# Two layers of a hybrid attention and mixture-of-experts trunk: when VectorE takes up layer 0's conditioning vectors, and in which PSUM bank they wait

## The reference, cut to what matters

```
m = silu(cvec) @ w_ada[li] + b_ada[li]          # split into 6 vectors of 1024
h = rmsnorm(y, g_pre_mix[li]) * (1 + m[1]) + m[0]
u = h @ w_in[li]                                # 1024 x 2560: q, k, v of both attentions, pool
y = y + m[2] * rmsnorm(attention_and_pool(u) @ w_out[li], g_post_mix[li])
h = rmsnorm(y, g_pre_ffn[li]) * (1 + m[4]) + m[3]
y = y + m[5] * rmsnorm(moe(h), g_post_ffn[li])  # 64 routed experts, top 8, and a shared one
```

## Time and profile before

| | |
|---|---|
| median of 3 runs | 1432.21 us (1431.74 to 1433.58) |
| profiled execution | 1431.63 us, of which its span 1429.8 us |
| TensorE busy | 1344.9 us, 94% of the span |
| VectorE busy | 466.5 us, 33% |
| ScalarE busy | 334.3 us, 23% |
| mean DMA rate | 348 GB/s |
| granted TensorE clock, mean | 0.972 of full |

### The profile page before, as it was taken

The page is one execution under the profiler, slowest core; times in us unless marked ns, Lnnn a source line. Parts: engine busy times, 40 slices in busy tenths (PEclk is TensorE's granted clock), DMA queues, the critical chain, the costliest instruction groups (busy, mean ns, idle before and its releaser), DMA issues.

```text
span 1429.8 us, 30290 instructions
## 1 busy us (share of the span) xinstructions
PE 1344.9 (94%) x12298; PEld 734.1 (51%) x12298; DVE 466.5 (33%) x1110; ACT 334.3 (23%) x594; POOL 64.7 (5%) x89
## 2 busy tenths in 40 slices
PE   3859989999999999999989998999999999999996
PEld 2646755445444544544547875544454454454453
DVE  0514754222222222222237375422222222222223
ACT  1413551111111111111134365111111111111111
POOL 0210020000000000000013102000000000000000
PEclk9889989999999999999999998999999999999999
DMA  9878465999999999999966846599999999999990
GB/s 368 330 297 334 174 251 200 396 404 412 398 406 412 393 418 401 404 401 405 409 235 222 323 175 260 195 385 416 410 394 417 408 401 400 412 408 403 398 410 31
DMA packets 86294, 497.42 MB, mean 348 GB/s; under 512 B 7728, under 2 KB 7728, under 8 KB 36336
## 3 DMA queue, kind: packets, MB, share of 16 engines
q1 hardware_dynamic: 84416, 491.58, 85.8%
q0 software_dynamic: 1840, 5.31, 1.0%
HBM read 494.24 MB, written 2.62 MB: 347 GB/s over the span
## 4 chain that ended last, share of the span: by engine, by line
PE 88%; DMA 3%; DVE 3%; ACT 2%; issue 1%; SPq 1%; POOL 1%; ACTq 0%; POOLq 0%
PE PS L877 31%; PE PS L908 16%; PE PS L852 12%; PE PS L680 9%; PE PS L869 9%; DMA weights<-in_w_in 3%; PE PS L701 2%; PE PS L820 2%; PE PS L896 1%; PE PS L841 1%; ACT weights_split L983 1%; PE PS L772 1%; SPq L388 1%; DVE h L1213 1%; PE PS L859 1%
## 5 line engine op out<-in xcount | busy, mean ns | idle before, releaser
L877 PE MATMUL PS<-weights,gathered 128*32 128x512 f32 (+1 forms) x3968 | 451.3, 592 | 0.0
L877 PEld LDWEIGHTS PS<-weights,gathered 128*32 128x32 f32 (+1 forms) x3968 | 133.6, 111 | 306.3 <-issue 306.3
L908 PE MATMUL PS<-weights,hiddenT 128*32 128x512 f32 (+1 forms) x1984 | 233.0, 595 | 0.0
L852 PEld LDWEIGHTS PS<-pick,x_parts 128*128 128x128 bf16 x3168 | 177.2, 98 | 54.7 <-issue 54.7
L852 PE MATMUL PS<-pick,x_parts 128*128 128x128 bf16 x3168 | 188.3, 219 | 0.0
L1538 DVE SCALAR_TENSOR_TENSOR hidden<-PS,slot_gate,silu 128x256 f32<-128x256 f32 x64 | 30.9, 484 | 397.8 <-ACT silu L1103 397.8
L1110 ACT ACTIVATE y_hi<-PS 128x512 fp32r<-128x512 f32 x128 | 76.5, 598 | 295.8 <-PE PS L908 295.8
L1548 DVE TENSOR_TENSOR y_lo<-PS,y_hi 128x512 fp32r<-128x512 f32 x128 | 88.5, 692 | 140.2 <-ACT y_hi L1110 140.2
L1103 ACT ACTIVATE silu<-PS 128x256 f32<-128x256 f32 x64 | 24.6, 384 | 417.5 <-PE PS L877 417.5
L908 PEld LDWEIGHTS PS<-weights,hiddenT 128*32 128x32 f32 (+1 forms) x1984 | 60.5, 110 | 116.0 <-issue 114.6
L680 PE MATMUL PS<-weights_split,hT_high 128*128 128x512 f32 x448 | 111.5, 403 | 7.7 <-ACT hT_high L964 6.1
(11 more groups left out here) (268 smaller groups left out, 952.8 us busy)
## 6 DMA issues: line engine op xcount, KB each, us to landing
weights<-in_w_gate SPq DMA_DIRECT2D x128, 1024.0 KB, 7.7
weights<-in_w_up SPq DMA_DIRECT2D x128, 1024.0 KB, 11.6
weights<-in_w_down SPq DMA_DIRECT2D x128, 1024.0 KB, 9.2
weights<-in_w_ada SPq DMA_DIRECT2D x24, 2048.0 KB, 13.8
weights<-in_w_in SPq DMA_DIRECT2D x9, 2048.0 KB, 11.2
weights<-in_w_out SPq DMA_DIRECT2D x4, 2048.0 KB, 10.3
weights<-in_w_in SPq DMA_DIRECT2D x2, 1024.0 KB, 24.2
weights<-in_ws_gate SPq DMA_DIRECT2D x2, 1024.0 KB, 5.5
```

What stands on the lines that cost most here:

```text
L852: last = mm(PS[:, 5 + half, j * P:(j + 1) * P], x3[:, g, part, jj, :], pick[:, u % 2, g, 0:P], start=(g, part) == (0, 0), stop=(g, part) = ...
L877: last = mm(PS[a:z, 4, :].rearrange("p (a n) -> p a n", a=2), xgT[:, b, j, a:z], w[:, e, :, j, :], start=j == 0, stop=j == KT - 1, tile_po ...
L908: last = mm(PS[a:z, bank, :], hidT[:, j, a:z], w[:, e, j, n * HALF:(n + 1) * HALF], start=j == 0, stop=j == FT - 1, tile_position=(0, a), ...
```

## The change

Three edits. In the in-projection loop the vector after block n goes to bank n % 2 and not to bank 0: (0,2) to bank 1, (0,3) to bank 0, (0,4) to bank 1. VectorE's `finish_vector` stands ahead of the low part of block n + 1 and reads the matching bank. The head transposes at the start of attention, which write banks 0 and 1, wait for the latest vector begun, not for the latest in bank 0; for layer 0 both are the fifth.

```diff
@@ attention(l), TensorE
-                if 0 in last_in:
-                    pe.wait_ge(mod_ready, last_in[0])
+                if AFTER_BLOCK[l]:
+                    pe.wait_ge(mod_ready, started[0])
                 heads_out(0, range(8), 0, 0)
@@ in-projection loop, TensorE
                     if n in AFTER_BLOCK[l]:
-                        modulate(AFTER_BLOCK[l][n], 0)
+                        modulate(AFTER_BLOCK[l][n], n % 2)
@@ in-projection loop, VectorE
                 for n in range(5):
+                    if n - 1 in AFTER_BLOCK[l]:
+                        finish_vector((n - 1) % 2)
                     if n < 4:
                         low_weights(l, "in", n + 1)
                     if l == 0 and n == 2:
                         lambda_sums()
                     if l == 0 and n == 4:
                         lambda_values()
-                    if n - 1 in AFTER_BLOCK[l]:
-                        finish_vector(0)
                     dve.wait_ge(u_mm, 10 * l + 2 * n + 2)
```

## The result

The changed kernel takes 1419.09 us (median of 4 runs, 1415.32 to 1420.57) against 1432.14 us before (median of 4, 1431.74 to 1433.58). The ratio is 0.9903 with a 95% interval of 0.9883 to 0.9923, so it is faster by 13 us, between 11 and 17 by the interval. The prediction was 1417.2, a gain of 15.0. The first median lies 0.6 us above the forecast's own range (1416 to 1418.5) and inside the outer one (1414.6 to 1421.5); the second lies in both.

What follows compares the result with a forecast made beforehand. TensorE bounds the kernel, held twice in layer 0's in-projection by VectorE's late `mod_raw`. Gain 16.5 less 1.5 for the clock is 15.0 us: 1431.63 becomes 1416.6, with the median 0.6 higher 1417.2; range 1416 to 1418.5, outer 1414.6 to 1421.5.

Steps and rivals of the forecast that it cites:

- the forecast's own range: Whole kernel: 1416 to 1418.5 us for the main case, a pause with a fall of the clock, given 54%.
- the outer one: Whole kernel: 1414.6 to 1421.5 us, taking in the first two rivals; about 2 in 10 lie outside.
- Bank 0 and not the weights holds (0,3)'s product; VectorE's order makes it late.: Layer 0's in-projection after block 2: TensorE idles 14.83 us until VectorE takes (0,2) out of bank 0.
- Either edit alone opens it, the second is worth 0.: At block 2's end, 79.50: the order or the banks alone frees (0,3)'s product; the other edit adds 0.
- Block 3's load is late next, 5.0 us of idle.: Ahead of block 3: weights land at 84.52, high part ends at 88.15, leaving TensorE 5.0 us idle.
- Clock term 1.5, bounds 0 and 2.0.: Block 3 after its pause: TensorE's clock falls and costs 1.5 us, between 0 and 2.0.
- The rival without a fall (25%): Block 3: pause too short for the clock to fall, gain 16.5 us, time 1415.7; chance 25%.
- Block 4's load in time by 0 to 2 us.: Ahead of block 4: load issued at 81.4, landed 97.7 to 100.2, hidden by 0 to 2 us.
- (1,0)'s second half in time by 2.7 us, by 0.7 with the writes.: Attention: this load's slack falls from 7.4 to 2.7 us, to 0.7 if key and value writes precede it.
- Everything from attention on moves as one piece.: Attention, router and expert loads hang on block 4's end, so all that follows shifts by the same amount.
- The sum.: Whole kernel: gain 16.5 us less 1.5 for the clock, 15.0 us, giving 1417.2 for the median.
- the spread of runs at 0.7 us: Whole kernel: 0.7 us allowed for differences between runs when setting the bounds 1414.6 to 1421.5.

Runs made afterwards that it cites:

- e2: Changed kernel with VectorE's new order alone, all three vectors staying in bank 0: 1418.34 us, ratio 0.9896 against the kernel before.
- e3: Changed kernel with the alternating banks alone, VectorE taking vectors up behind the low part as before: 1419.18 us, ratio 0.9903 against the kernel before.
- e1: The changed kernel run again, nothing altered, beside the kernel before at 1433.05 us: 1417.0 us, ratio 0.9885.
- e4: Changed kernel plus 40 unread matmuls in TensorE's pause ahead of block 3 of layer 0: 1416.43 us.
- e6: Changed kernel with vectors (0,3) and (0,4) after blocks 3 and 4 instead of 2 and 3, so block 3's load goes first: 1416.56 us.
- e7: Changed kernel plus unread matmuls in four pauses: ahead of layer 0's block 3, ahead of block 0 in both layers, behind (1,2)'s product: 1414.77 us.
- e5: Changed kernel with block 4's load in layer 0 issued only when group 0 of block 3's product is through: 1425.1 us, ratio 0.995.
- e9: Changed kernel with (0,3) after block 3, (0,4) and (0,5) within attention, (1,0) with (1,1) after the out-projection: 1407.92 us, ratio 0.9831.
- e10: Order of e9 plus unread matmuls ahead of block 0 in both layers and behind (1,2)'s product: 1403.89 us, ratio 0.9808.

## Why the prediction was right, point by point

- *Bank 0 and not the weights holds (0,3)'s product; VectorE's order makes it late.* Right: with either remedy (e2, e3) the wait is gone.
- *Either edit alone opens it, the second is worth 0.* Right, by e2 and e3.
- *Block 3's load is late next, 5.0 us of idle.* Right: 5.62 here, 5.28 in e1, 5.50 in e2. Of the 0.6 too little in the first, 0.35 is the load (18.2 us from issue to landing rather than 17.9) and 0.25 the time from the end of ScalarE's high part (90.23) to the first matmul (90.48), which the sum had at nothing.
- *Clock term 1.5, bounds 0 and 2.0.* The fall came in every profiled execution in which the pause was left empty. Its size was 6.04 - 3.93 = 2.1 us (2.2 in e1, 1.6 in e2, 2.15 in e3), so the term was too small by 0.6, and its upper bound by 0.2. I took it from the shortest of three rows; the two longer ones were nearer. The rival without a fall (25%) didn't occur; e4 shows what it would have been worth. Its condition, a pause shorter than the 5.3 us after which the clock fell before, doesn't hold: by the 0.81 of 84.8 to 90.4 the clock fell at about 88.3, 3.4 us after TensorE had stopped.
- *Block 4's load in time by 0 to 2 us.* Right, by 2.3 us (105.74 against 108.05).
- *(1,0)'s second half in time by 2.7 us, by 0.7 with the writes.* Right in sign, nearly used up: issued at about 107.5 it landed 23.1 us later, at 130.6, and TensorE reached it at 131.0 (129.16 + 1.8). I had carried over the landing of the last half from before, 24.5 us after block 3's end; it was 26.8, with key and value writes and the out-projection's load now issued 11 us before it lands where that was 4 us. e6 shows what lies on the other side of that margin. That nothing was lost here is partly luck: 0.3 us were left, in e1 0.8. The rows in the changed kernel's first profile, the product's from the timeline and the load's from the DMA issues at 107.5:

```profile
129.16 3.66 PE L701 MATMUL PS<-weights,c_columns 128*32 128x256 f32 x64
...
weights<-in_w_ada SPq DMA_DIRECT2D x1, 2048.0 KB, 23.1
```

The Trainium skill (DMA: Bandwidth & Descriptors, Queues, rings and completion order) has the queues take turns packet by packet. The landings fit that: the four writes, issued from 118.5 on, had landed by 129.4, ahead of this load issued at 107.55, and it came 7.4 us behind the half before it where that was 5.4 in the kernel before. But no run here leaves the key and value writes out, so their share isn't shown.
- *Everything from attention on moves as one piece.* The experts do, to 0.02 us. The stage before them is 0.97 us shorter. By the rows 0.5 of it lies ahead of the out-projection, where 16 transposes (L519) took 1.92 us here and 3.16 before (granted clock 1.00 in 146 to 156 here, 0.83 in 158 to 168 before), and 0.45 in the router's 16 matmuls behind a pause, 5.62 us here and 6.07 before. It is no gain of the change: e4 and e7, with the same order of work, have the 107.6 and 107.7 of before in that column.
- *The sum.* The stage itself gave 13.97 us for a forecast of 15.0 (14.19 in e1, 14.63 in e2, 14.04 in e3): the idle time was 0.6 longer and the clock term 0.6 larger. That the two stages together come to 14.9 is luck, since the 0.97 of the second aren't the change's. The median moved by 13.05 in the first comparison and by 16.05 in the second (1433.05 - 1417.0); one kernel's runs scatter by as much as 5 us (1415.3 to 1420.6 changed, 1430.2 to 1435.6 before), so that the median of 1417.0 falls on the forecast of 1417.2 says little. The lower end of the outer range is 0.2 off its own terms: 1432.2 - 16.7 - 0.7 is 1414.8.

That scatter is what the prediction underrated: it put the spread of runs at 0.7 us. Several falls of the clock lie in each execution at pauses that the change doesn't touch (block 0 of both layers, the router), and the one at layer 0's block 0 alone costs 1.3 to 2.8 us over 3.93. The Trainium skill (TensorE: Matmul & The Clock Gate, What's actually happening) says that this stretch varies from run to run and advises against fitting to one figure, since it is under 1% of a typical kernel. The trace agrees with the first (5.3 to 6.7 us for one and the same 16 matmuls), and a single fall is under 1% here as well (2.8 of 1420 us); but where the change itself is worth 1% and several falls come together, that is no comfort.

Layer 1's attention, which differs by up to 1.5 us between executions (106.27 to 107.75), is of the same kind by its rows: the router's 16 matmuls there took 6.56 us in the changed kernel's first profile and 5.25 in e1, 5.76 before, and the granted clock in the 8 us ahead of them was 0.53 in the first profile (866 to 874) and 0.75 in the 6.5 us ahead of them in e1 (866 to 872.5). What stays open is why one execution gets its clock back sooner than another, and whether the 1.3 us more in layer 1's in-projection, which come with the change in nearly every trace, are chance.

## What to carry to other kernels

A late reader of a PSUM bank costs more than its wait where weights go through a ring: the late product holds a ring place, and the next load starts late with it (e5: 6 to 8 us). Once this stage was free of such waits its limit was the order of its loads, and what one of them gained another lost, unless the late one went to a stage where TensorE stood idle anyway (e6 lost its gain, e9 kept it). Differences of 1 to 2 us are read between fixed marks in the trace and not from totals, which scatter with the clock; unread work in a pause keeps the clock up (e4, e7, e10). That it narrows the spread of the runs isn't shown: they lie within 1.5 us in e10 and 2.6 in e7, but within 1.4 in e3 and 1.7 in e5, which have nothing filled.

## What the runs showed of the hardware

- Unread matmuls of about 4 us ahead of block 0 brought the granted clock in 41 to 46 us from 0.50 or 0.71 to 1.00, and one pause filled with 40 of them kept it at 1.00, so that the 16 matmuls behind it took 3.90 us and not 5.5 to 6.1 (e4).
- The time from issue to landing of a 2 MB load was 7.7 us alone, and 18.2 with two others ahead of it, 18.8 and 23.1 with three in the changed kernel (the last beside the key and value writes as well): it follows what is queued, so a margin taken from a trace in which the queue was shorter is too large.
